# Recurrent branch: the products of masked key weights with values moved behind the last Horner product

## The reference

```python
def step(s, inp):
    r_t, w_t, k_t, v_t, kk_t, a_t = inp
    sa = jnp.einsum('bhij,bhj->bhi', s, -kk_t)
    s = (s * w_t[:, :, None, :] + sa[..., None] * (kk_t * a_t)[:, :, None, :]
         + v_t[..., None] * k_t[:, :, None, :])
    return s, jnp.einsum('bhij,bhj->bhi', s, r_t)
```

## Time and profile before

| | |
|---|---|
| median of 3 runs | 2697.28 us (2697.2 to 2699.13) |
| the profiled execution | 2701.25 us, span 2699.3 us |
| mean granted clock of TensorE | 0.990 |
| TensorE products busy | 2575.0 us (95%) |
| VectorE busy | 1257.5 us (47%) |
| ScalarE busy | 884.2 us (33%) |
| GpSimd busy | 181.9 us (7%) |

### The profile page before, as it was taken

How to read it: one execution, slowest core, us unless ns; L and a number is a source line. 1 busy time by engine, 2 the same in 40 slices (tenths; PEclk the granted TensorE clock), 3 DMA queues, 4 the chain that set the end, 5 groups by cost and what they waited for, 6 DMA issues and landing times.

```text
span 2699.3 us, 49718 instructions
## 1 busy us (share of the span) xinstructions
PE 2575.0 (95%) x21572; PEld 1737.6 (64%) x21572; DVE 1257.5 (47%) x2466; ACT 884.2 (33%) x1438; POOL 181.9 (7%) x164
## 2 busy tenths in 40 slices
PE   7999999999999999999999999999999999999997
PEld 3675857667566565666656767585866656666665
DVE  3453526355387445222335455454638745332323
ACT  2323314242345544211024242433325545431111
POOL 0000000000000002112310000000000000021222
PEclk9999999999999999999999999999999999999998
DMA  8102021110201000211321010101001100012122
GB/s 296 49 18 81 18 81 32 72 42 18 81 32 36 25 17 16 109 63 57 105 95 41 7 45 2 42 10 34 18 27 32 36 26 16 24 39 73 63 69 78
DMA packets 34838, 136.60 MB, mean 51 GB/s; under 512 B 4480, under 2 KB 4512, under 8 KB 33984
## 3 DMA queue, kind: packets, MB, share of 16 engines
q1 hardware_dynamic: 31248, 118.18, 12.9%
q0 software_dynamic: 3376, 15.24, 1.6%
HBM read 126.43 MB, written 6.98 MB: 49 GB/s over the span
## 4 chain that ended last, share of the span: by engine, by line
PE 84%; DVE 8%; ACT 5%; issue 2%; DMA 1%; POOL 0%; SPq 0%; ACTq 0%; DVEq 0%; POOLq 0%
PE psum L579 82%; PE psum L582 2%; DVE tmp L1545 1%; DVE m_nm L2037 1%; DVE tmp L1548 1%; DMA ring<-units 1%; ACT tmp L1249 1%; DVE acts L1545 1%; ACT tmp L1498 1%; DVE tmp L1556 1%; DVE tmp L1552 1%; ACT L1244 0%; DVE tmp L1931 0%; ACT L1240 0%; DVE tmp L1859 0%
## 5 line engine op out<-in xcount | busy, mean ns | idle before, releaser
L579 PE MATMUL psum<-hT,ring 128*128 128x512 f32 (+2 forms) x3264 | 946.1, 442 | 8.3 <-DVE hT L1553 4.9
L579 PEld LDWEIGHTS psum<-hT,ring 128*128 128x128 f32 x3264 | 525.7, 192 | 415.2 <-issue 372.5
L579 PE MATMUL psum<-tmp 64*64 64x64 f32 (+9 forms) x10624 | 700.7, 258 | 42.9 <-DVE tmp L1548 12.5
L579 PEld LDWEIGHTS psum<-tmp 64*64 64x64 f32 (+3 forms) x10624 | 550.7, 149 | 159.4 <-issue 56.3
L1249 ACT ACTIVATE tmp<-psum 128x512 f32<-128x512 f32 (+7 forms) x490 | 252.4, 518 | 1037.8 <-PE psum L579 963.5
L1249 ACT ACTIVATE acts<-psum 128x640 f32<-128x640 f32 (+4 forms) x206 | 109.4, 531 | 322.0 <-PE psum L579 299.5
L579 PE MATMUL psum<-acts,ring 128*128 128x512 f32 (+1 forms) x768 | 210.8, 434 | 0.0
L1545 DVE TENSOR_TENSOR tmp<-psum,tmp 128x256 f32<-128x256 f32 (+2 forms) x184 | 75.7, 411 | 258.7 <-PE psum L579 189.9
L1545 DVE TENSOR_TENSOR tmp<-tmp,psum 128x320 f32<-128x320 f32 x120 | 56.3, 486 | 264.6 <-PE psum L579 202.6
L579 PEld LDWEIGHTS psum<-acts,ring 128*128 128x128 f32 x768 | 118.6, 191 | 94.7 <-issue 92.1
L1545 DVE TENSOR_TENSOR tmp<-tmp 128x320 f32<-128x320 f32 (+2 forms) x214 | 135.1, 658 | 5.0
(11 more groups left out here) (162 smaller groups left out, 2176.2 us busy)
## 6 DMA issues: line engine op xcount, KB each, us to landing
ring<-units SPq DMA_DIRECT2D x210, 512.0 KB, 3.5
small_sb<-small SPq DMA_DIRECT2D x1, 2944.0 KB, 11.0
small_sb<-small POOLq DMA_DIRECT2D x1, 2944.0 KB, 10.3
hT<-xT SPq DMA_DIRECT2D x2, 1280.0 KB, 7.1
tmp<-xT POOLq DMA_DIRECT2D x8, 320.0 KB, 5.1
x_keep<-hT POOLq DMA_DIRECT2D x8, 320.0 KB, 4.2
tmp<-x_keep POOLq DMA_DIRECT2D x8, 320.0 KB, 3.4
yT<-acts POOLq DMA_DIRECT2D x8, 320.0 KB, 3.2
```

The lines of the kernel that those rows point to most:

```text
L579: return nc.tensor.matmul(out, lhsT, rhs, start=start, stop=stop, skip_group_check=True)
```

## The change

On TensorE the AV product of the first step of each group leaves its place ahead of N, and that of the other step its place ahead of V2. Both are issued behind V3 of all steps of the group and ahead of the opening of state and output. ScalarE's copies of both come, in its order, behind its copies of N.

```diff
@@ TensorE
                         beat(4)
-                        weighed_values(steps[0])
                         for s in steps:
                             got(s, ("T16", "act"))
...
                             block(s, "V1", "dve", B(s, "E"), B(s, "H", 8)[:, 0:4, :])
-                        for s in steps[1:]:
-                            weighed_values(s)
                         beat(6)
...
                             block(s, "V3", "dve", B(s, "E"), B(s, "G"))
+                        for s in steps:
+                            weighed_values(s)
                         open_outputs(steps[0])
```

## The result

The changed kernel takes 2715.75 us (median of 5 runs, 2707.21 to 2721.56) against 2697.28 for the kernel before in the same comparison (5 runs, 2696.8 to 2703.47): ratio 1.0059, interval 1.0035 to 1.0082. That is 18.5 us slower by the medians, where +1.5 was forecast. Run again beside other kernels it came to 2712.12 against 2699.01: 1.0043 (1.0031 to 1.0056). So it is slower for certain, by 0.3 to 0.8%, and part of the first figure is not the change's, as will be seen.

What follows compares the result with a forecast made beforehand. TensorE's order of work was taken as the bound, its products holding 82% of the chain. 16 x 0.09 + 8 x 0.00 = +1.5 us on the median 2697.28 gave 2698.8 us, range 2695 to 2703.

Steps and rivals of the forecast that it cites:

- the chain in the groups of two: TensorE, two-step groups: 0.62 us of new waits, then sixteen AV instructions in a row; 6.75 us becomes 6.84.
- +0.09 for each group: Added time per two-step group up to open's second instruction; 16 such groups give +1.5 us.
- no gain from fewer changes of mode: Two-step groups: four mode changes fewer would give 0.54 us a group, but 0.62 of new waits stand against it.
- the rival "faster": Two-step groups: mode switches are saved and the gaps do not open; 8.6 us gained, time 2688.7, chance 0.06.
- step 4 as a piece of TensorE's work: One-step group: 0.84 us saved ahead of N, 0.84 added behind V3; sum 0.00, eight times.
- the modulation row: Layer 0, step 4, ScalarE: its copy comes later behind AV's copy but stays hidden, its reader coming after Ya; 0 cost.
- the banks: PSUM bank assignment: unchanged in two-step groups, shifted by a ticket elsewhere; at most 0.05 + 0.39 us, taken as 0.
- the third rival: Shifted banks put a wait of about 0.4 us into each two-step group; 7.9 us, time 2705.2, chance 0.06.
- 1.5 + 0 + 0: Forecast sum: 16 x 0.09 for two-step groups, 8 x 0.00 for step 4, and 0 for the banks.

Runs made afterwards that it cites:

- m_pairs: Against the kernel before, AV moved only in the 16 two-step groups, step 4 left as before; costs 3.6 us at equal clock.
- m_four: Against the kernel before, AV moved only in the one-step group (step 4), 8 products; costs 5.1 us at equal clock.
- b_banks: Kernel before, no product moved, bank ages behind each layer's recurrent branch set to the changed kernel's; costs 4.7 us.
- x_banks: Changed kernel, bank ages behind both layers' recurrent branches set to the kernel before's in layer 0; 2697.43 us, +3.7 at equal clock.
- m_first: Against the kernel before, only AV of each group's first step moved behind V3, step 4 included; +9.9 us at equal clock.
- x_fix: Changed kernel with the kernel before's layer 0 bank ages in both layers, and ScalarE's modulation-row copy ahead of AV's copies again; 2701.15 us.
- b_best: Kernel before, no product moved, its own layer 0 bank ages set behind the recurrent branch of both layers; 2694.79 us, ratio 0.9982.
- c_before: The kernel before, run again unchanged as a control; ratio 1.0004 against itself.

## Why the prediction was wrong

**Right: the chain in the groups of two.** The waits, their places and the run of 16 are as worked out, and the two halves add up as their chains say (0.15 + 0.06). The term was mis-sized: "+0.09 for each group" measured +0.21, from a sum that starts 0.07 late and an open that is 0.05 slower to its second instruction. It comes to 16 x 0.21 = 3.4 in place of 1.5; m_pairs, where only this was done, shows 3.6. In the changed kernel the total is 2.5: in every other pair the group (2, 3) began with a bank wait of 0.33 before, which mostly goes. That is step 4's doing and not that of the groups, since m_four lacks these waits as well (-1.2) and m_pairs keeps them.

**Right: no gain from fewer changes of mode.** The Trainium skill, TensorEngine Tiling (Array Packing), Key Properties, says that a change of tiling mode drains the engine. The runs agree that a change has its price and that it is saved here: the sixteen AV instructions go 0.11 apart with one entry and one exit. By the prices in the rows, without the waits, the gain would have been 8.6 us. But the new waits are worth more in every group, and the rival "faster" fell by them.

**Right: step 4 as a piece of TensorE's work.** In layer 1, where no row is copied there, three such stretches sum to 236.59 us in the changed kernel and 236.69 before (singly 0.2 shorter, 0.3 longer and 0.2 shorter). The forecast was 0.00.

**Wrong: the modulation row.** The prediction says that the copy "comes later; the product that reads it comes after Ya, so it stays hidden". I asked who needs what the copy writes, and not who needs what it sets free. The next user of its bank waits for it as well: the wait of 0.46 us in the row above, 0.53 later a time, 2.1 us in the four pairs of layer 0.

**Wrong, and the largest part: the banks.** "Elsewhere the assignment shifts by a ticket. A bank met too early would cost up to one copy, 0.05 + 0.39; I take 0." The rule was replayed for the groups of two alone, where nothing does shift, and the third rival looked for the wait in the same place. It had the mechanism right and its place and price wrong: 3.3 us in a branch that the change does not touch, from single waits of up to 2.02, over four times the bound that I gave (0.44). The timeline says why: the reader there is not a copy behind a short product but a 0.82 us instruction that stands in VectorE's order behind other work. The expectations for b_banks and m_four took the 5.4 us of the view for the price, and that for x_banks the 7.3 of all five waits.

**The sum and what stays open.** 2.5 + 3.3 + 2.5 = 8.3 by the traces, where 1.5 + 0 + 0 was forecast, and 9.7 at equal clock with a standard error of 0.8. In m_first and b_banks the measured loss is further above the sum (9.9 for 7.4, 4.7 for 3.3), and that part stays open. Of the 18.5 us of the first comparison the rest is mostly clock: its runs had a mean of 0.989, where before had 0.991 in the second comparison, and 4 us of it stood ahead of any changed code in the profiled one. Whether the changed kernel also tends to a lower clock because of its waits is not shown; what the profiles have on it is told below. The groups were not repaired any further: with both bank causes gone (x_fix) the change is still 1.9 us slower at equal clock (standard error 0.6), and b_best, the kernel before with good banks, has the lowest median of all.

## What to carry to other kernels

Where buffers are given out in turn by one counter, a product that is moved shifts every later assignment, in branches that it never touches: replay the whole order of buffers to the end of the program, not the stretch around the edit, and look for a user whose new buffer has a slow reader. Of a copy that comes later ask two things, who needs what it writes and who needs the buffer that it empties. And when an edit changes the time by more than its own stretch can hold, compare the totals of waits by what released them first; the line whose count went from 3 to 7 was the largest part of the answer. But price a new wait by how much later the same products start, since it can stand in the place of an old one. Here setting the order of the buffers by hand, with nothing else changed, proved the cause and gave a faster kernel.

## What the runs showed of the hardware

Short waits for a bank were often followed by a low clock. Two stretches of layer 1, the changed kernel (second run) right behind its wait of 2.02 us at 2164.98, and b_best over the whole of the same part:

```profile
2165.00:2172.00 7.00, 7.00 (x32) 4.59 (x34) 4.82 (x12) 0.74 (x1) 0.00 (x0) 0.52 0.01 2
```

```profile
2140.00:2190.00 50.00, 48.41 (x373) 33.66 (x371) 32.02 (x65) 22.07 (x28) 1.52 (x3) 1.00 0.12 38
```

TensorE is busy all of the first stretch and yet at 0.52, that is 1.2 GHz for nearly all of it; before the fall stands only the wait, and the small products behind it. Ten profiles have this wait (1.84 or 2.02 us), and eight of them show 3.4 to 6.8 us at 1.2 GHz that begin at most 1.5 us behind it, a ninth shows them 14 us behind it; the tenth (b_banks) shows none, and neither do the three kernels without the wait (x_banks, x_fix, b_best). By the slope above 3.4 us at 1.2 GHz cost some 1.5 us (the same products of layer 1 take 34.1 us in c_before and 35.8 in b_best, which has 3.4 us at 1.2 GHz among them), so a wait of 2 us can be worth about twice its length. The same wait in layer 0 (2.02 at 865.35) was followed by it in three of six profiles only. The Trainium skill, TensorE: Matmul & The Clock Gate, What's actually happening, puts the clock down to how busy TensorE has been of late. Eight of the ten profiles fit that, with a wait of no more than 2.02 us; b_banks, with the same wait and no fall, shows that the wait alone does not decide it.
